# One encoder layer on one core: first norm's root moved behind the input projection, front loads cut in column blocks

## Chip, core and metric

The kernel runs on one core of one Trainium2 chip. The metric is the device time of the core in microseconds (us), lower is better. Before: 941.05 us, median of three runs (940.95 to 941.78).

## What is computed

One layer over 256 tokens of width 2048, all in fp32 (cut):

```python
xn = rmsnorm(x, norm_mix)                   # x * rsqrt(mean(x*x)+eps) * gain
p = xn @ w_in                               # 2048 x 6400, 25 units of 256 columns
yA = rwkv7_mixer(pA, ...)                   # first 7 units: token mix, LoRA, decay, state
yB = chunk_band_attention(pB)               # 6 units, 8 heads
yC = diff_attention(pC)                     # 6 units, 4 heads
yD = short_conv_mixer(pD)                   # 6 units
x = x + concat(yA, yB, yC, yD) @ w_out
x = x + hier_moe(rmsnorm(x, norm_ffn), ...) # group + top-2 of 32 experts, 192 MB of weights
return rmsnorm(x, norm_final)
```

## The kernel before

Each engine has its program, written out by hand; semaphores join them. An fp32 product is made of three float32r products: ScalarE rounds the weights (`split_hi`, L653), VectorE subtracts to get the rest (`split_lo`, L1715), TensorE forms high x high, low x high and high x low. **x** is treated likewise (`x_high` L614, `x_low` L1703).

TensorE goes through `w_in` in **granules**, a quarter of a unit's 2048 rows: 24 products of 256 columns (L1046; L1003 and L1016 in the first unit). I number them from 0: unit n is granules 4n to 4n+3, the projection 0 to 99. A granule needs `split_lo` of its number; `split_hi` of granule g needs granule g-4 used up. So both splits run three to four granules ahead at most. `advance(k)` on ScalarE and `split_lo(k)` on VectorE set by hand where splits stand between other work. Results go alternately to two PSUM banks `PJ`; unit n+2 may start when unit n is read out.

At the start VectorE and ScalarE square x (L1675, L599), GpSimd takes the root (L498), x is multiplied by it (L601, L1685, L1691) and then transposed by TensorE (L965). TensorE runs idle products until then (`warm`, L970).

Units 0 to 6 feed the RWKV mixer: `keep(n)` (ScalarE, L671) stores one share, `mix(n)` (VectorE, L1723) adds the shifted one. Between stand the LoRA products after granule 11 (L1090 to L1096, read by ScalarE L694, L697, L586), the squares' sum after granule 17 (L1103, read by ScalarE L713 after a table load), VectorE's scan (L1759), four reciprocals (L1771) and `prep_done` (L1798), for which TensorE waits after granule 32 (L1111). Units 7 to 24 are read out by ScalarE (`evac`, L586).

SyncE issues nearly all loads in one queue, in the order written. A weight load of unit n waits for granules of unit n-2. Expert units of 2 MB (one of 3 x 32 matrices) go to ten slots `wslot`; from the output projection on these are filled as memory comes free, then each as the experts release it. After the last expert the tail squares, takes two roots (GpSimd) and scales and stores both token blocks.

## Time and profile before

| | us |
|---|---|
| median of three runs | 941.05 |
| the profiled execution | 941.73 |
| its span, first to last instruction | 939.9 |
| TensorE busy | 784.9 (84%) |
| VectorE busy | 432.2 (46%) |
| ScalarE busy | 279.7 (30%) |

Times in the rows count from the start of the span. A granule or a group stands in the chain of waits when nothing later held back its end. TensorE's granted clock is 0.925 of full speed over the whole; up to 520 us each stretch shows 1.00.

### The profile page before, as it was taken

The page shows a single profiled execution, that of the slowest core. Times are in us where ns is not written, and L with a number is a line of the kernel's source. Part 1 is how long each engine was busy: PE and PEld are TensorE (multiplying, and loading weights), DVE is VectorE, ACT ScalarE, POOL GpSimd, SP SyncE. Part 2 cuts the span into 40 slices and gives each one's busy share as a digit, 9 for nine tenths or more (in the row PEclk, how much of TensorE's full clock was granted, in tenths as well). Part 3 has the DMA queues.
Part 4 walks back from the last instruction along what each step waited for, and adds up shares of the span by engine and source line. Part 5 has one row for each costly group of instructions (what it writes and reads, how often), then busy time and mean ns, then how long its engine had stood idle before and what let it go on. Part 6 is the DMA issues. An engine that isn't in the chain of part 4 may idle for free.

```text
span 939.9 us, 18496 instructions
## 1 busy us (share of the span) xinstructions
PE 784.9 (84%) x8182; PEld 633.8 (67%) x8182; DVE 432.2 (46%) x710; ACT 279.7 (30%) x457; POOL 72.3 (8%) x78
## 2 busy tenths in 40 slices
PE   8999999999999999999999775675746856468654
PEld 7999999999999999888877352343513534235332
DVE  6758947654676576845452412114131132311403
ACT  6555543433355656455410000000010000100014
POOL 3110003250000000800000000000000000000002
PEclk9999999999999999999999987798787977979778
DMA  9695544434344455799989999999999999999994
GB/s 301 208 286 153 179 133 137 128 102 135 119 148 140 136 158 178 257 344 382 383 333 412 427 427 429 426 428 425 428 426 430 424 430 425 428 427 425 428 399 178
DMA packets 84799, 285.83 MB, mean 304 GB/s; under 512 B 3834, under 2 KB 55300, under 8 KB 72300
## 3 DMA queue, kind: packets, MB, share of 16 engines
q1 hardware_dynamic: 82448, 279.20, 76.8%
q0 software_dynamic: 1568, 4.02, 1.6%
q8 instruction: 66, 1.08, 0.5%
q10 hardware_dynamic: 700, 1.39, 0.4%
q14 instruction: 17, 0.14, 0.0%
HBM read 280.37 MB, written 4.22 MB: 303 GB/s over the span
## 4 chain that ended last, share of the span: by engine, by line
PE 60%; DMA 32%; DVE 4%; ACT 2%; issue 1%; SPq 0%; POOL 0%; DVEq 0%; ACTq 0%; POOLq 0%
PE bank L1046 26%; DMA arena<-in_expert_w_up 12%; DMA arena<-in_expert_w_down 10%; DMA arena<-in_expert_w_gate 9%; PE bank L1510 8%; PE bank L1590 3%; PE bank L1063 3%; PE bank L1065 3%; PE bank L1064 3%; PE bank L965 2%; PE bank L1475 2%; PE bank L1209 1%; DVE ring_r L1715 1%; PE bank L1016 1%; PE bank L1602 1%
## 5 line engine op out<-in xcount | busy, mean ns | idle before, releaser
L1046 PE MATMUL bank<-xTr,hi 128*128 128x256 f32 x1280 | 235.7, 286 | 0.3 <-DVE ring_r L1715 0.2
L1510 PE MATMUL bank<-arena 128*32 128x256 f32 x2048 | 140.7, 442 | 106.2 <-DMA arena<-in_expert_w_up 62.9
L1046 PEld LDWEIGHTS bank<-xTr,hi 128*128 128x128 f32 x1280 | 199.3, 192 | 5.4 <-issue 3.3
L1715 DVE TENSOR_TENSOR ring_r<-arena,hi 128x1024 fp32r<-128x1024 f32 x132 | 161.8, 1236 | 87.6 <-ACT hi L653 85.1
L1510 PEld LDWEIGHTS bank<-arena 128*32 128x32 f32 x2048 | 79.2, 127 | 165.8 <-issue 137.2
L1046 PE MATMUL bank<-xTr,ring_r 128*128 128x256 f32 x640 | 181.0, 283 | 0.0
L653 ACT ACTIVATE hi<-arena 128x1024 fp32r<-128x1024 f32 x132 | 138.8, 1062 | 115.1 <-PE bank L1046 84.3
L1046 PEld LDWEIGHTS bank<-xTr,ring_r 128*128 128x128 f32 x640 | 122.7, 192 | 0.0
L2149 DVE TENSOR_TENSOR arena<-arena,bank 128x512 f32<-128x512 f32 x56 | 57.9, 1093 | 72.8 <-PE bank L1486 72.8
L894 ACT ACTIVATE g<-bank,coef 128x256 f32<-128x256 f32 x8 | 3.8, 473 | 255.1 <-PE bank L1510 255.1
L1590 PE MATMUL bank<-arena,const 128*32 128x512 f32 x448 | 54.3, 640 | 16.6 <-DMA arena<-in_expert_w_down 16.6
L2176 DVE SCALAR_TENSOR_TENSOR lora<-g,bank 128x256 f32<-128x256 f32 x8 | 3.4, 421 | 134.1 <-ACT g L894 134.1
L1475 PEld LDWEIGHTS bank<-Sel,arena 128*128 128x128 f32 x512 | 58.6, 192 | 4.4 <-issue 3.7
L1475 PE MATMUL bank<-Sel,arena 128*128 128x128 f32 x512 | 60.9, 277 | 0.4 <-issue 0.4
L2153 DVE TENSOR_TENSOR yg<-bank,yg 128x512 fp32r<-128x512 f32 x32 | 21.4, 686 | 82.6 <-ACT yg L879 82.6
L1063 PE MATMUL bank<-hi,yTr 128*128 128x512 f32 x128 | 50.4, 394 | 0.0
L1065 PE MATMUL bank<-ring_r,yTr 128*128 128x512 f32 x128 | 49.9, 390 | 0.0
L1064 PE MATMUL bank<-hi,yTr 128*128 128x512 f32 x128 | 49.8, 389 | 0.0
L1590 PEld LDWEIGHTS bank<-arena,const 128*32 128x32 f32 x448 | 17.6, 117 | 47.4 <-issue 47.4
L586 ACT ACTIVATE arena<-bank 128x512 f32<-128x512 f32 (+4 forms) x67 | 32.2, 481 | 54.4 <-PE bank L1186 23.5
L1046 PE MATMUL bank<-hi,xTr 128*128 128x256 f32 x256 | 47.8, 288 | 0.0
L879 ACT ACTIVATE yg<-bank 128x512 fp32r<-128x512 f32 x32 | 18.4, 597 | 89.5 <-PE bank L1590 71.2
(339 smaller groups left out, 885.6 us busy)
## 6 DMA issues: line engine op xcount, KB each, us to landing
arena<-in_expert_w_gate SPq DMA_DIRECT2D x30, 2048.0 KB, 29.7
arena<-in_expert_w_up SPq DMA_DIRECT2D x29, 2048.0 KB, 31.6
arena<-in_w_in SPq DMA_DIRECT2D x50, 1024.0 KB, 5.3
arena<-in_expert_w_down SPq DMA_DIRECT2D x24, 2048.0 KB, 30.3
arena<-in_w_out SPq DMA_DIRECT2D x16, 1024.0 KB, 7.8
arena<-in_expert_w_down SPq DMA_DIRECT2D x16, 512.0 KB, 8.9
arena<-in_expert_w_down SPq DMA_DIRECT2D x8, 1024.0 KB, 15.2
arena<-in_expert_w_up SPq DMA_DIRECT2D x6, 1024.0 KB, 6.3
```

Of the source, the lines that this page charges most:

```text
L586: step(A_(dst, src, ACT.Copy, **kw), signal)
L653: A_(hi[:, g % NHI, :], ring[:, n % 2, q, :], ACT.Copy).then_inc(s["hi_done"], 1)
L1046: ins = MM(PJ[n % 2][:, h * U:(h + 1) * U], a, b, start=h + q + tt + k == 0, stop=h == 1 and q == 3 and tt == 3 and k == 2)
L1063: MM(o_, yTr[:, 0, t, tok], wh[:, tt, :], start=t == 0, stop=False)
L1064: MM(o_, yTr[:, 1, t, tok], wh[:, tt, :], start=False, stop=False)
L1065: ins = MM(o_, yTr[:, 0, t, tok], wl[:, tt, :], start=False, stop=t == KT - 1)
L1475: ins = MM(bk[:, k * P:(k + 1) * P], src[:, m, t, :], Sel[:, m, :], start=m == 0, stop=m == NM - 1)
L1510: ins = MM(gu[slots_of(a), u * EH:(u + 1) * EH], xg[:, t, slots_of(a)], slot(NUQ * h + NCG * u + a)[:, t * EH:(t + 1) * EH], start=t == 0, ...
L1590: ins = MM(bank[4 + n][slots_of(a), :], hT[:, k, slots_of(a)], slot(NUQ * h + 2 * NCG + a)[:, k * DM + n * 512:k * DM + (n + 1) * 512], st ...
L1715: TT(ring_r[:, n % 2, q, :], ring[:, n % 2, q, :], hi[:, g % NHI, :].bitcast(f32), ALU.subtract).then_inc(s["lo_done"], 1)
L2149: TT(t, t, bk[:, :].rearrange("p (q t) -> p q t", t=KT), ALU.add).then_inc(s["sct_ev"], 1)
L2153: TT(buf[:, 1, :], bank[4 + n][:, :], buf[:, 0, :].bitcast(f32), ALU.subtract).then_inc(s["yg_lo"], 1)
```

## The change

- The first norm's root is no longer applied to x. x is transposed as it comes. The squares are taken later; a product of ones with a diagonal of the two roots (after granule 6) gives `R`, the root along the free axis. VectorE multiplies each mixer unit in PSUM by `R` (`scale(n)`) before `keep` and `mix` read it; the read-out of units 7 to 24 moves from ScalarE to VectorE and multiplies by the root.
- x and the first unit's weights are loaded in four pairs of 512 KB by SyncE, behind the identity matrix; TensorE takes x block by block between the first granules. The parameter loads on GpSimd wait for the last x block.
- The first expert unit is loaded one step of SyncE's loop earlier, behind a wait for the last transposed probabilities; the slots at 64 and 112 KB change places. The router's weights and gains are loaded during attention.
- Tail: the second root is taken before the first block is scaled, GpSimd and ScalarE take all four column blocks of the second token block, stored in two halves.
- In `mix`, one `split_lo` stands between `scale` and the mixing; single ones are taken out elsewhere, the one between the reciprocals among them.

```diff
@@ -363,9 +367,12 @@
 
         @block.sync
         def _(sp):
-            sp.dma_start(xs[:, 0, :], x_v[0]).then_inc(x_ld[0], 16)
-            for n, part in ((1, slice(0, DM // 2)), (2, slice(DM // 2, DM))):
-                sp.dma_start(xs[:, 1, part], x_v[1][:, part]).then_inc(x_ld[n], 16)
+            sp.dma_start(const[:, 0:P], A["const"][:, 0:P]).then_inc(const_ld, 16)
+            for q in range(4):
+                cols_ = slice(q * 512, (q + 1) * 512)
+                sp.dma_start(xs[:, :, cols_], x_cols[:, :, cols_]).then_inc(x_ld[q], 16)
+                sp.dma_start(ring[:, 0, q, :].rearrange("p (t c) -> p t c", t=4),
+                             w_in_v[:, 4 * q:4 * q + 4, order[0] * U:(order[0] + 1) * U]).then_inc(part_ld[q], 16)
...
@@ -407,10 +414,12 @@
...
-                if NU_IN + 2 <= n < NU_IN + 7:
+                if NU_IN < n < NU_IN + 6:
+                    if n == NU_IN + 1:
+                        sp.wait_ge(s["pt_ps"], NBH + NCH)
                     if n == NU_IN + 3:
                         sp.wait_ge(s["ylo_done"], YD1)
-                    moe_unit(0, n - NU_IN - 2)
+                    moe_unit(0, n - NU_IN - 1)
...
@@ -468,13 +477,11 @@
             for lo, up in ((0, 1), (1, 2), (2, 4)):
                 sp.wait_ge(s["go"], up)
                 store_out(0, lo * 512, up * 512)
-            sp.wait_ge(s["go"], 5)
-            store_out(1, 1536, 2048)
...
@@ -500,10 +507,12 @@
...
+            step(G.memset(ones_f, 1.0), s["pool_ones"])
+            pool.wait_ge(s["xt_ready"], 8)
+            for dst, src in loads:
+                pool.dma_start(dst, src).then_inc(par_ld, 16)
             rsqrt(st[:, 0:1])
             rsqrt(st[:, 1:2])
-            for dst, src in loads:
-                pool.dma_start(dst, src).then_inc(par_ld, 16)
...
@@ -545,6 +554,11 @@
...
+            pool.wait_ge(s["sm_done"], sm_count(NBH - 1))
+            pool.dma_start(gain_tp[:, :], cols(A["norm_ffn"])).then_inc(par2_ld, 16)
+            pool.dma_start(gain_pt[:, :], A["norm_ffn"].rearrange("l (p t) -> p (l t)", t=KT)).then_inc(par2_ld, 16)
+            pool.dma_start(rw[:, :, 0:NGR], A["router_group_w"].rearrange("l (t p) g -> p (l t) g", t=KT)).then_inc(par2_ld, 16)
+            pool.dma_start(rw[:, :, NGR:36], A["router_expert_w"].rearrange("l (t p) g -> p (l t) g", t=KT)).then_inc(par2_ld, 16)
             for i in range(NCH):
                 rsqrt(cst[:, :, 1:2])
...
@@ -614,32 +620,7 @@
...
-            def evac(n):
-                act.wait_ge(s["gran_used"], 4 * n + 4)
...
-                if n < NA + 12 and i < 2:
-                    copy(dst, src.rearrange("p (a m t) -> p a m t", a=2, m=2), s["pj_evac"], scale=HD ** -0.5)
-                else:
-                    copy(dst, src.rearrange("p (a b) -> p a b", a=2), s["pj_evac"])
-
-            pos = {"split": 0, "pe": 0}
...
@@ -671,11 +651,17 @@
...
-            for b in range(8):
-                if b % 2 == 0 and b < 2 * LEAD:
-                    split_hi()
-                x_high(b)
-            advance(4)
+            for q in range(4):
+                x_high(2 * q)
+                x_high(2 * q + 1)
+                split_hi()
+            split_hi()
+            square(0)
+            split_hi()
+            square(1)
+            split_hi()
+            act.wait_ge(gain_ld, 16 * NVECS + 1)
+            A_(vec[:, KT:NVEC], K[1][:, 0:NVEC - KT], ACT.Copy).then_inc(gain_ld, 1)
             keep(0)
             act.dma_start(const[:, P:], A["const"][:, P:]).then_inc(const_ld, 16)
             advance(1)
...
@@ -946,15 +932,14 @@
...
-            act.wait_ge(s["z_done"], 3)
             act.wait_ge(s["sq3_done"], 8)
-            for n in range(3):
+            for n in range(4):
+                act.wait_ge(s["z_done"], max(3, n + 1))
                 cols_ = slice(n * 512, (n + 1) * 512)
                 A_(x2n[:, 1, cols_], x2z[:, cols_], ACT.Copy, scale=st[:, 1:2]).then_inc(s["sq3_done"], 1)
-            act.wait_ge(s["sq3_done"], 10)
-            act.dma_start(out_v[1][:, 0:1024], x2n[:, 1, 0:1024]).then_inc(out_st, 16)
-            act.wait_ge(s["sq3_done"], 11)
-            act.dma_start(out_v[1][:, 1024:1536], x2n[:, 1, 1024:1536]).then_inc(out_st, 16)
+                if n % 2 == 1:
+                    act.wait_ge(s["sq3_done"], 9 + n)
+                    act.dma_start(out_v[1][:, (n - 1) * 512:(n + 1) * 512], x2n[:, 1, (n - 1) * 512:(n + 1) * 512]).then_inc(out_st, 16)
@@ -979,25 +964,23 @@
...
-            warm(26)
-            pe.wait_ge(s["scaled0"], 1)
-            for b in range(7):
-                if b == 4:
-                    pe.wait_ge(s["scaled0"], 2)
-                    pe.wait_ge(gain_ld, 16 * NVECS)
-                    nc.tensor.transpose(PJ[0][:, 0:NVEC], vec_nat, ident[0:NVEC, 0:NVEC]).then_inc(gain_ld, 1)
-                x_transpose(b, 0)
-            for b in range(7):
-                pe.wait_ge(s["scaled1"], b // 4 + 1)
-                x_transpose(b, 1).then_inc(s["xt_ready"], 1)
+            pe.wait_ge(gain3_ld, 16)
+            nc.tensor.transpose(PJ[0][:, 0:KT], gain_nat, ident[0:KT, 0:KT]).then_inc(gain3_ld, 1)
+
+            def x_block(q):
+
+                pe.wait_ge(x_ld[q], 16)
+                for b in (2 * q, 2 * q + 1):
+                    if b == 7:
+                        pe.wait_ge(s["xlo_done"], 2)
+                    x_transpose(b, 0)
+                    x_transpose(b, 1).then_inc(s["xt_ready"], 1)
 
...
@@ -1017,12 +1000,15 @@
...
+            x_block(0)
+            x_block(1)
             for q in range(4):
                 first_high(q)
                 first_low(q)
-                if q == 0:
-                    x_transpose(7, 0)
-                    x_transpose(7, 1).then_inc(s["xt_ready"], 1)
+                if q < 2:
+                    x_block(q + 2)
+            pe.wait_ge(gain_ld, 16 * NVECS)
+            nc.tensor.transpose(K[1][:, 0:NVEC - KT], vec_nat, ident[0:NVEC - KT, 0:NVEC - KT]).then_inc(gain_ld, 1)
...
@@ -1077,7 +1063,13 @@
...
-            granules(4)
+            granules(3)
+            pe.wait_ge(s["diag_done"], NM)
+            pe.wait_ge(s["pool_ones"], 3)
+            for m in range(NM):
+                ins = MM(K[2][:, m * P:(m + 1) * P], ones_f, diag[:, m, :], start=True, stop=True)
+            ins.then_inc(s["ones_ps"], 1)
+            granules(1)
...
@@ -1670,31 +1662,6 @@
...
-            half = slice(DM // 2, DM)
-            step(TS(xs[:, 0, half], xs[:, 0, half], st[:, 0:1], None, ALU.mult), s["scaled0"])
-            v.wait_ge(s["sq1_done"], 2)
-            step(TT(st[:, 1:2], st[:, 1:2], st[:, 2:3], ALU.add))
-            variance(1)
-            v.wait_ge(s["rstd_done"], 2)
-            for half in (slice(0, DM // 2), slice(DM // 2, DM)):
-                step(TS(xs[:, 1, half], xs[:, 1, half], st[:, 1:2], None, ALU.mult), s["scaled1"])
-            v.wait_ge(gain_ld, 16 * NVECS + 2)
...
@@ -1704,6 +1671,29 @@
...
+            def evac(n):
+                v.wait_ge(s["gran_used"], 4 * n + 4)
...
+                if n < NA + 12 and i < 2:
+                    step(STT(dst, PJ[n % 2][:, :].rearrange("p (a m t) -> p a m t", a=2, m=2), HD ** -0.5,
+                             R[:, :].rearrange("p (m t) -> p m t", m=2).unsqueeze(1).to_broadcast([P, 2, 2, P]), ALU.mult,
+                             ALU.mult), s["pj_evac"])
+                    return
+                by = st[:, 0:NM].unsqueeze(2) if order[n] in natural else R[:, :].unsqueeze(1)
+                step(TT(dst, PJ[n % 2][:, :].rearrange("p (a b) -> p a b", a=2), by.to_broadcast([P, 2, U]), ALU.mult),
+                     s["pj_evac"])
...
@@ -1714,22 +1704,54 @@
...
+                    if q == 3 and NA <= n - 1 < NU_IN - 1:
+                        evac(n - 1)
...
+            def scale(n):
+
+                v.wait_ge(s["gran_used"], 4 * n + 4)
+                t = PJ[n % 2][:, :].rearrange("p (h t) -> p h t", h=2)
+                step(TT(t, t, R[:, :].unsqueeze(1).to_broadcast([P, 2, SEQ]), ALU.mult), s["pj_scaled"])
 
             def mix(n):
 
+                scale(n)
+                split_lo(1)
                 for h in range(2):
                     i = 2 * order[n] + h
                     v.wait_ge(s["mix1"], 2 * n + 2)
                     step(STT(mA[:, i, 1:], PJ[n % 2][:, h * SEQ:(h + 1) * SEQ - 1], mu[:, i:i + 1], mA[:, i, 1:],
                              ALU.mult, ALU.add), s["mixA"])
 
-            for b in range(8):
-                x_low(b)
-                if b % 2 == 1 and b < 2 * LEAD:
-                    split_lo(1)
-            split_lo(4)
+            for q in range(4):
+                x_low(2 * q)
+                x_low(2 * q + 1)
+                split_lo(1)
+            split_lo(1)
+            square(0)
+            split_lo(1)
+            square(1)
+            split_lo(1)
+            v.wait_ge(s["sq1_done"], 2)
+            step(TT(st[:, 0:NM], st[:, 0:NM], st[:, NM:2 * NM], ALU.add))
+            for m in range(NM):
+                variance(m)
+            for m in range(NM):
+                v.wait_ge(s["rstd_done"], m + 1)
+                step(TS(diag[:, m, :], ident, st[:, m:m + 1], None, ALU.mult), s["diag_done"])
+            v.wait_ge(gain_ld, 16 * NVECS + 2)
+            step(TS(omu[:, :], mu, -1.0, 1.0, ALU.mult, ALU.add), s["prep"])
+            step(TS(w0h, w0h, 0.5, None, ALU.mult), s["prep"])
+            step(TS(a0h, a0h, 0.5, None, ALU.mult), s["prep"])
+            step(TS(ok_a[:, :], k_a, -1.0, 1.0, ALU.mult, ALU.add), s["prep"])
+            v.wait_ge(s["ones_ps"], 1)
+            step(V.tensor_copy(R[:, :], K[2][:, 0:SEQ]))
             mix(0)
-            split_lo(1)
...
@@ -1745,12 +1767,12 @@
             mix(1)
             for c in range(2):
                 step(TS(kk[:, c, :], k_[:, c, :], k_k[:, c:c + 1], None, ALU.mult))
-            split_lo(4)
+            split_lo(3)
             mix(2)
             for c in range(2, 4):
                 step(TS(kk[:, c, :], k_[:, c, :], k_k[:, c:c + 1], None, ALU.mult))
             step(TT(kmod, kk, kk, ALU.mult), s["kr_done"])
-            split_lo(2)
+            split_lo(1)
             flat = [t.rearrange("p a b -> p (a b)") for t in (decay, chunk_start, Pc)]
             step(V.memset(chunk_start, 1.0))
             step(TS(iclr, iclr, 0.5, 0.5, ALU.mult, ALU.add))
             split_lo(1)
             mix(3)
-            split_lo(1)
             split_lo(2)
             v.wait_ge(s["knorm_done"], 2)
...
             mix(4)
             for c in range(AT):
                 step(V.reciprocal(kmod[:, c, :], kmod[:, c, :]))
-                if c == 1:
-                    split_lo(1)
             split_lo(1)
             step(TT(kk, kk, kmod, ALU.mult), s["kr_done"])
             split_lo(1)
...
             mix(5)
-            split_lo(1)
             step(V.memset(flat[1][:, 0::CH], 1.0))
             split_lo(1)
...
             step(TT(iclr, iclr, kk, ALU.mult))
-            split_lo(1)
             step(TT(bh, iclr, Pinv, ALU.mult))
...
@@ -2223,16 +2240,12 @@
             add_last(3)
             v.wait_ge(s["sq3_done"], 7)
             variance3(0)
-            v.wait_ge(gain3_ld, 16)
-            v.wait_ge(s["rstd_done"], NRSTD - 1)
-            scale_psum(0)
             v.wait_ge(s["sq3_done"], 8)
             variance3(1)
-            for n in range(1, 4):
+            v.wait_ge(gain3_ld, 34)
+            v.wait_ge(s["rstd_done"], NRSTD - 1)
+            for n in range(4):
                 scale_psum(n)
-            v.wait_ge(s["rstd_done"], NRSTD)
-            cols_ = slice(3 * 512, 4 * 512)
-            STT(x2n[:, 1, cols_], x2n[:, 1, cols_], st[:, 1:2], gain3[:, cols_], ALU.mult, ALU.mult).then_inc(s["go"], 1)
             assert step.count[s["var_ready"]] == NRSTD
```

**ScalarE, after the first unit** (L653 and L637 are `split_hi`; L671 and L651 `keep`; L613 the squares). Before:

```order
L614 ACTIVATE xTr<-bank,vec 128x256 x8
L653 ACTIVATE hi<-arena 128x1024 x4
L671 ACTIVATE arena<-bank,omu 128x256 x2
L680 DMA const<-in_const 128x992
L653 ACTIVATE hi<-arena 128x1024
L683 ACTIVATE arena<-arena 64x256
```

and now:

```order
L637 ACTIVATE hi<-arena 128x1024 x2
L613 ACTIVATE arena,st<-arena 128x1024
L637 ACTIVATE hi<-arena 128x1024
L613 ACTIVATE arena,st<-arena 128x1024
L637 ACTIVATE hi<-arena 128x1024
L664 ACTIVATE vec<-bank 128x46
L651 ACTIVATE arena<-bank,omu 128x256 x2
L666 DMA const<-in_const 128x992
L637 ACTIVATE hi<-arena 128x1024
L669 ACTIVATE arena<-arena 64x256
```

Seven splits stand before `keep(0)` both times; `keep(0)` now waits for `scale(0)`, and that for the product with ones.

**VectorE, from the fourth to the fifth mixer unit** (L1715 and L1705 are `split_lo`, L1723 and L1728 `mix`, L1719 `scale`). Before:

```order
L1767 TENSOR_SCALAR arena<-arena 128x1024
L1715 TENSOR_TENSOR ring_r<-arena,hi 128x1024
L1723 SCALAR_TENSOR_TENSOR arena<-bank,vec,arena 128x255 x2
L1771 RECIPROCAL arena<-arena 128x256 x2
L1715 TENSOR_TENSOR ring_r<-arena,hi 128x1024
L1771 RECIPROCAL arena<-arena 128x256 x2
L1715 TENSOR_TENSOR ring_r<-arena,hi 128x1024
L1775 TENSOR_TENSOR arena<-arena 128x1024
```

and now:

```order
L1788 TENSOR_SCALAR arena<-arena 128x1024
L1705 TENSOR_TENSOR ring_r<-arena,hi 128x1024
L1719 TENSOR_TENSOR bank<-bank,Sel 128x512
L1705 TENSOR_TENSOR ring_r<-arena,hi 128x1024
L1728 SCALAR_TENSOR_TENSOR arena<-bank,vec,arena 128x255 x2
L1792 RECIPROCAL arena<-arena 128x256 x4
L1705 TENSOR_TENSOR ring_r<-arena,hi 128x1024
L1794 TENSOR_TENSOR arena<-arena 128x1024
```

The split of granule 23 has moved ahead of the mixing and all four reciprocals now stand before that of granule 24.

**VectorE, from the third mixer unit to the scan** (L1752 and L1774 the squares of k, L1759 and L1781 the scan). Before:

```order
L1723 SCALAR_TENSOR_TENSOR arena<-bank,vec,arena 128x255 x2
L1751 TENSOR_SCALAR arena<-arena,vec 128x256 x2
L1752 TENSOR_TENSOR arena<-arena 128x1024
L1715 TENSOR_TENSOR ring_r<-arena,hi 128x1024 x2
L1755 MEMSET arena 128x1024
```

and now:

```order
L1719 TENSOR_TENSOR bank<-bank,Sel 128x512
L1705 TENSOR_TENSOR ring_r<-arena,hi 128x1024
L1728 SCALAR_TENSOR_TENSOR arena<-bank,vec,arena 128x255 x2
L1773 TENSOR_SCALAR arena<-arena,vec 128x256 x2
L1774 TENSOR_TENSOR arena<-arena 128x1024
L1705 TENSOR_TENSOR ring_r<-arena,hi 128x1024
L1777 MEMSET arena 128x1024
```

The mixing and the squares now stand behind the split of granule 15.

## Rows read from the trace of the kernel before

**Rows 1.** The page, chain that ended last, shares by engine.
```profile
PE 60%; DMA 32%; DVE 4%; ACT 2%; issue 1%; SPq 0%; POOL 0%; DVEq 0%; ACTq 0%; POOLq 0%
```

**Rows 2.** Chain of waits, 0 to 130 us: start, length, what.
```profile
0.73 5.38 DMA arena<-in_x
...
15.07 1.19 PE bank L1003 x8
...
27.66 11.52 PE bank L1046 x96
...
60.80 1.07 ACT hi L653
...
69.91 3.14 PE bank L1046 x24
73.05 1.74 PE bank L1103 x8
...
98.30 20.42 PE bank L1046 x168
118.72 1.68 PE bank L1111 x16
```

**Rows 3.** The same chain, in the experts.
```profile
523.82 21.50 DMA arena<-in_expert_w_up
...
869.22 32.90 DMA arena<-in_expert_w_up
```

**Rows 4.** Timeline, 0 to 15 us: start, length, engine, line, operation.
```profile
1.41 6.96 PE L970 MATMUL bank<-ones 128*128 128x128 bf16 x78 [1.41 <-POOL ones L502]
...
13.40 1.57 ACT L614 ACTIVATE xTr<-bank,vec 128x256 fp32r<-128x256 f32 x4
```

**Rows 5.** VectorE's groups, 27 to 120 us: busy us, mean ns.
```profile
L1715 DVE TENSOR_TENSOR ring_r<-arena,hi 128x1024 fp32r<-128x1024 f32 x31 | 37.7, 1224 | 17.1 <-ACT hi L653 16.4
L1771 DVE RECIPROCAL arena<-arena 128x256 f32<-128x256 f32 x4 | 7.0, 1751 | 0.1
L1723 DVE SCALAR_TENSOR_TENSOR arena<-bank,vec,arena 128x255 f32<-128x255 f32 x14 | 6.7, 480 | 3.0 <-ACT arena L671 2.7
L1759 DVE TENSOR_TENSOR_SCAN arena<-arena 128x1024 f32<-128x1024 f32 x1 | 2.3, 2291 | 0.0
...
L1755 DVE MEMSET arena<- 128x1024 f32 x1 | 0.9, 912 | 0.2 <-issue 0.2
...
L1751 DVE TENSOR_SCALAR arena<-arena,vec 128x256 f32<-128x256 f32 x2 | 0.7, 353 | 0.1
L1758 DVE TENSOR_SCALAR arena<-arena 128x1024 f32<-128x1024 f32 x1 | 0.7, 694 | 0.0
```

**Rows 6.** Timeline of ScalarE, 39 to 78 us.
```profile
39.21 0.84 ACT L671 ACTIVATE arena<-bank,omu 128x256 f32<-128x256 f32 x2 [1.75 <-PE bank L1046]
...
74.86 1.28 ACT L713 ACT_TABLE_LOAD   x1 [1.03 <-PE bank L1103]
76.16 1.23 ACT L713 ACTIVATE arena<-bank 128x512 f32<-128x512 f32 x2
```

**Rows 7.** VectorE on 128x512 with one side in PSUM: timeline at 147 us.
```profile
147.88 0.68 DVE L1822 TENSOR_TENSOR arena<-bank,const 128x512 f32<-128x512 f32 x1
```

**Rows 8.** The page, costliest groups: the same form in the experts.
```profile
L2149 DVE TENSOR_TENSOR arena<-arena,bank 128x512 f32<-128x512 f32 x56 | 57.9, 1093 | 72.8 <-PE bank L1486 72.8
```

**Rows 9.** Windows: from:to, us, busy of each engine, PEclk, DMA share, GB/s.
```profile
250.00:300.00 50.00, 50.00 (x460) 47.19 (x459) 35.75 (x77) 27.92 (x51) 1.64 (x1) 1.00 0.45 144
380.00:385.00 5.00, 5.00 (x34) 4.55 (x33) 2.65 (x5) 2.72 (x4) 4.64 (x5) 1.00 0.48 157
485.00:490.00 5.00, 4.64 (x46) 4.06 (x48) 4.26 (x22) 0.37 (x2) 0.00 (x0) 1.00 1.00 364
490.00:495.00 5.00, 5.00 (x76) 3.32 (x65) 2.93 (x12) 0.00 (x0) 0.00 (x0) 1.00 0.80 273
```

**Rows 10.** Timeline of the tail: GpSimd's root, ScalarE's and VectorE's scaling, last store.
```profile
932.05 0.55 POOL L498 TENSOR_TENSOR st<-st,mhalf 128x1 f32<-128x1 f32 x1 [1.28 <-DVE st L2207]
932.64 1.95 ACT L953 ACTIVATE arena<-arena,st 128x512 f32<-128x512 f32 x3 [2.12 <-POOL st L498]
933.92 0.74 DVE L2235 SCALAR_TENSOR_TENSOR arena<-arena,st 128x512 f32<-128x512 f32 x1
...
934.61 0.38 ACTq L957 DMA_DIRECT2D out<-arena  x1
```

More of the change, by code:

```diff
@@ L243, in build @@
         t5_dram = nc.dram_tensor("t5_scratch", [4, SPAN], f32)
-        x_ld = [sem(f"x_ld{m}") for m in range(NM + 1)]
+        x_ld = [sem(f"x_ld{m}") for m in range(3)]
         gain_ld, par_ld, par2_ld, par3_ld, const_ld = (sem(n) for n in ("gain_ld", "par_ld", "par2_ld", "par3_ld", "const_ld"))
@@ L252, in build @@
         x2_st = [sem(f"x2_st{n}") for n in range(4)]
-        tail_ld = [sem(f"tail_ld{n}") for n in range(3)]
+        part_ld = [sem(f"part_ld{n}") for n in range(3)]
         gain3_ld, x2o_ld, out_st = sem("gain3_ld"), sem("x2o_ld"), sem("out_st")
+        x_ld.append(x2o_ld)
+        part_ld.append(out_st)
         rel_st, bias_ld = sem("rel_st"), sem("bias_ld")
@@ L383, in store_x2 @@
                 sp.dma_start(x2_cols[:, :, nb * 512:(nb + 1) * 512], x2b[nb % 3]).then_inc(x2_st[nb], 16)
-            for n in range(NU_IN + NU_OUT):
+            for n in range(1, NU_IN + NU_OUT):
                 for half in range(2):
@@ L818, in _ @@
             advance(1)
-            advance(NG_IN - pos["pe"] + 3)
+            advance(NG_IN - (pos["split"] - LEAD) + 3)
             act.wait_ge(s["dconv0"], 1)
@@ L845, in _ @@
             for nb in range(3):
-                advance(NG_IN + 8 * (nb + 1) - pos["pe"])
+                advance(NG_IN + 8 * (nb + 1) - (pos["split"] - LEAD))
                 square_block(nb)
@@ L851, in _ @@
                 rows_permuted(nb)
-            advance(NG - pos["pe"])
+            advance(NG - (pos["split"] - LEAD))
             act.wait_ge(s["wo_ev"], 7)
@@ L1452, in _ @@
             MM(bank[5][:, 0:NE], ones[:, :], em[:, 0, :], start=True, stop=False)
-            MM(bank[5][:, 0:NE], ones[:, :], em[:, 1, :], start=False, stop=True).then_inc(s["total_ps"], 1)
+            MM(bank[5][:, 0:NE], ones[:, :], em[:, 1, :], start=False, stop=True).then_inc(s["ones_ps"], 1)
             def sel_transpose(q):
@@ L1839, in _ @@
                 if i in (1, 2):
-                    step(V.memset(S[i - 1], 0.0), s["halves_zero"])
+                    step(V.memset(S[i - 1], 0.0), s["diag_done"])
                 if i == 3:
```

124 lines of the change are left out of this document (49 added, 75 removed).

## The prediction

> **What bounds the kernel now.** I read the shares of the chain first, then the chain in order of time, then the groups and the timeline of VectorE and ScalarE between 27 and 120 us, the windows around the start of the experts, and the tail. TensorE holds 60% of the chain and DMA 32% [rows 1]: up to about 520 us TensorE sets the pace, after that the stream of expert weights [rows 3], which runs without a break until its last wait ends at 902.1 (869.22 + 32.90). The stream cannot start before TensorE has gone through both projections and the router, since the ten slots are full by then. So whatever moves TensorE's path before 500 us moves the end by as much, and the change has to be judged by that path.
>
> On it, the first product stands at 15.07, the first unit ends at 27.66, and a granule takes 2.88 us (11.52 for 96 products, four granules) [rows 2]. Four marks show how little room VectorE has in the mixer: the split behind ScalarE's at 60.80 leads to granule 17 at 69.91; the squares' sum ends at 74.79 (73.05 + 1.74); granule 26 starts at 98.30 behind VectorE; granule 33's predecessor ends and the bonus sums start at 118.72 [rows 2]. TensorE's need of granule 24 is 74.79 + 6 x 2.88 = 92.1. VectorE's busy share of 46% over the whole says nothing here.
>
> **The change, part by part.** A minus is earlier.
>
> 1. *The start.* Removed are squares, two roots and the scaling of x ahead of the transposes. Now TensorE makes 52 idle products instead of 78, to 1.41 + 52 x 0.089 = 6.05 [rows 4]; the first x block, 0.57 MB with the identity, should have landed by then, as the first 1 MB took 5.38 [rows 2]. Then transposes and the gain 0.5, four scaled copies 1.57 [rows 4], a split 1.07 [rows 2], handovers 0.3: first product at 9.5. From first product to the end of the unit it was 12.6 (15.07 to 27.66); twelve more transposes stand between, at most 0.12 each as a product of twice their width, so 14.0 at most, and 13.0 if the gaps of before close. I take 13.7, end 23.2: -4.5 (bounds -5.2 and -4.0).
>
> 2. *Granule 7.* This is where the new dependency bites. ScalarE's split of granule 7 stands behind `keep(0)`, that behind `scale(0)`, that behind the copy of `R`, that behind the product with ones after granule 6. After granule 6 TensorE waits for: ones 0.4, copy of R 0.4 (priced as one 256-wide PSUM read, half of 0.84 in rows 6), scale 0.69, keep 0.84 [rows 6], split on ScalarE 1.07, split on VectorE 1.22 [rows 5], five handovers of 0.05 or so and the issue of a load: 5.0. The scale writes PSUM, which no row shows; the nearest are 0.68 [rows 7] and, for the same width among the experts, 1.09 [rows 8]. I take 0.69, for rows 7 is from the stage of the mixer; with 1.09 seven scales cost 2.8 more, which is in the range. +5.0. Granule 8 follows behind mix 0.96, two activations 0.84, both splits 2.3 and gaps 0.3, 4.4 together, against 2.88 and the small T5 product 0.7 on TensorE: +0.8. The first three terms leave +1.3: the start is given back.
>
> 3. *Granule 17.* Before, mix, the two products with k_k and the squares of the third unit stood ahead of ScalarE's LoRA work, in free time. Now mix stands behind the split of granule 15, which ScalarE makes at 60.80 only [rows 2]. From there: splits 15 and 16, memset 0.91, 0.69, scan 2.29, split 17 gave 69.7, what the chain shows. Inserted are 0.96 + 0.71 + 1.22 = 2.9 [rows 5]. Covered by nothing: +2.8.
>
> 4. *Granules 24 to 26*, counted as if 1 to 3 had not been. Splits 17 and 18 end at 71.5. scale(3) 0.69, keep(3) 0.84; then ScalarE has three exponentials with splits 19 and 20 between (each 1.07 as a 1024-wide split) and a small one: 78.6. Table load 1.28 and roots 1.23 [rows 6]: 81.1, where before they began at 74.86 with the sum. Split 21 on both engines 83.4, maximum 0.69, split 22 85.3, scale(4) 86.0, keep 86.8, split 23 89.1, mix 90.1, four reciprocals at 1.75 and gaps [rows 5] 97.4, split 24 98.6. TensorE wants it at 92.1. Granule 26 follows at 104.4 against 98.30: +6.1. The split that stood between the reciprocals was what held 92.1; with scale(4) tied to the end of granule 19, even without the lateness the split 24 would come 1.8 too late.
>
> 5. *To the bonus sums.* VectorE from split 26 on: seven splits 8.5, two scales 1.4, twice the wait for keep and ScalarE's split 3.8, mixes 1.9, four 256-wide operations 2.0, five of 1.22, small ones 0.5: 24.2. So 128.5 against 118.72, of which 6.1 is counted: +3.6.
>
> 6. *The rest of the projection.* Eighteen read-outs at 0.69 go to VectorE. TensorE is not late anywhere here before, VectorE is busy 72% in the attention [rows 9]. Hidden mostly by three granules of lead, 8.6 us; if that cover is gone a read-out can cost its 0.69, all of them 12. I take +1.0 (0 to 4).
>
> 7. *The first expert unit* is issued some 10 us earlier, when the queues are half idle (share 0.48 [rows 9]), and it no longer crowds the output projection; the wait for the probabilities is over by the time SyncE reaches it, so nothing behind it in SyncE's queue is late. But it frees no slot: at 490 to 495 the DMA share drops to 0.80, the slots being full and waiting for the experts. An emptier queue earlier makes that gap longer. 0. The router's loads in attention: four issues on GpSimd ahead of the third kind of root, hidden; 0.
>
> 8. *The tail.* The second root ended at 932.60 [rows 10], now right behind the first at 931.6. ScalarE's three scalings move 1.0 earlier, a fourth (0.65) and an issue of 0.38 come in; VectorE loses 0.74. The last issue, 934.6 before [rows 10], stays within 0.2, but more is on its way by then: -0.6 (0 to -1.5).
>
> Sum: -4.5 + 5.8 + 2.8 + 6.1 + 3.6 + 1.0 - 0.6 = +14.2. The profiled execution took 941.73, its span and 1.8 around it; 955.9. It lies 0.7 above the median of the runs, so against them I say **955.2**.
>
> **The rivals.** (a) *The early expert unit pays after all*, the stream starting with less outstanding. For it: the share is 1.00 at 485 to 490. Against: the gap behind it. 2.1 MB at the 364 GB/s of that window are 5.8 us: 949.4. (b) *Attention runs dry too*: read-outs delay the softmax on VectorE and TensorE waits at each head, 4 us more: 959. For it: 72%. Against: TensorE's products fill its path there without a pause. (c) *The front's small loads are slow*: x block 3 lands late. If each of the four pairs took the 5.38 of the first 1 MB, the last is there at 22.2, and the unit ends behind transposes, copies, two splits and 24 products, 7.2 later, at 29.4: 6 us more, 961. Against it: the rate before did not wait for one transfer to end before the next. The Trainium skill, DMA: Bandwidth & Descriptors, section Bandwidth, asks for batches of 1 MiB or more, for three quarters of the peak; by that rule the 512 KB blocks speak against this change, and no row here shows one alone. (d) *The other side*: the leads hold. VectorE stood idle 17.1 us ahead of its splits between 27 and 120 [rows 5]. If that idle time takes up the scales, keeps and moved mixes, and the `R` product is ready so that granule 7's split is in time, only the start and tail count: 941.05 - 5.1 = 935.9. It decides at granule 24: if its split is there within 92.1 less the gain. Against: the idle time lies where VectorE waits for ScalarE, which now waits for VectorE. (e) *Gains and losses cancel* (the change does in effect nothing): the waits return only what the start gives, 941.
>
> **How the numbers follow.** Forecast 0.66, (a) 0.09, (b) 0.08, (c) 0.03, (d) 0.10, (e) 0.04. Around the forecast, the bounds of the terms (start, PSUM price, read-outs, tail) and a margin of a few tenths per chained step give 950 to 960. Taking in (a) and (b) and leaving out (c), (d) and (e): **946 to 961**. About 0.2%, 1.9 us, is what a measurement can tell from no change: faster 0.10, same 0.04, slower 0.86 (forecast, a, b, c).
>
> **What would show it.** First product at 9 to 10, first unit done by 24. A stall of TensorE of about 5 us before granule 7 in the chain, with ScalarE's `keep` and both splits; one of near 3 before granule 17; VectorE's four reciprocals in the chain and a stall of 6 before granule 24; `prep_done` ahead of the bonus sums at 132. The start of the output projection and every expert wait some 15 later than before, at equal spacing. Wrong would be: no reciprocals in the chain, or the last expert wait ending before 905.

## The result, and the profile after

The changed kernel takes 960.34 us (median of four runs, 959.54 to 961.26) against 941.24 in the same session, a ratio of 1.0197 (1.0184 to 1.021). The prediction said 955.2, range 946 to 961; its own bounds for the forecast, 950 to 960, were just passed. The profiled execution took 960.65, its span is 958.7, 18.8 longer than before. TensorE's granted clock is 0.923 over the whole (0.925 before).

The chain of waits of the changed kernel up to the attention, its longest pieces (start us, us, what; L1032 is the granule's product, L1719 `scale`, L637 and L1705 the splits, L699 ScalarE's table load, L1792 the reciprocals, L1103 the bonus sums, L950 transposes behind them). It answers to [rows 2]:

```profile
23.42 8.83 PE bank L1032 x72
...
33.26 0.71 DVE bank L1719
34.72 1.06 ACT hi L637
35.88 1.24 DVE ring_r L1705
37.16 5.33 PE bank L1032 x24
...
43.22 11.71 PE bank L1032 x96
...
84.88 1.28 ACT L699
...
96.31 1.76 DVE arena L1792
98.10 1.76 DVE arena L1792
99.88 1.76 DVE arena L1792
101.67 1.76 DVE arena L1792
...
109.65 1.23 DVE ring_r L1705
110.88 0.62 DVE bank L1719
...
134.81 1.95 PE bank L1103 x16
136.76 4.17 PE bank L950 x24
140.92 8.79 PE bank L1032 x72
```

Between 58.8 and 134.8 us no piece is TensorE's; before, it had those from 69.91 to 74.80 and from 98.30 to 118.72. Two pieces have the wrong length for their work. Granule 7 takes 5.33 us for 24 products where a granule takes 2.88, and the 24 transposes behind the bonus sums take 4.17 where they took 2.68. The windows say why (columns: stretch, length, busy us and count of TensorE, its weight load, VectorE, ScalarE, GpSimd, granted clock, DMA share, GB/s):

```profile
32.00:37.00 5.00, 0.69 (x7) 0.50 (x5) 2.25 (x3) 1.78 (x3) 0.00 (x0) 0.83 0.77 257
37.00:43.00 6.00, 5.84 (x26) 5.21 (x26) 4.76 (x14) 3.78 (x5) 0.42 (x1) 0.57 0.01 2
...
97.00:110.00 13.00, 8.20 (x49) 7.99 (x48) 11.48 (x9) 3.46 (x5) 0.00 (x0) 0.75 0.40 132
...
138.00:140.00 2.00, 2.00 (x11) 2.00 (x10) 0.30 (x1) 1.97 (x3) 0.00 (x0) 0.50 0.00 0
```

TensorE stood still from 32.7 to 37.16. At 36 to 37 us its granted clock was 0.50, which is 1.2 GHz, and it came back to 1.00 (2.4 GHz) between 42 and 43:

```profile
36.00:37.00 1.00, 0.00 (x0) 0.00 (x0) 1.00 (x1) 0.00 (x0) 0.00 (x0) 0.50 0.73 298
...
42.00:43.00 1.00, 1.00 (x6) 0.37 (x4) 0.97 (x2) 0.00 (x0) 0.42 (x1) 0.91 0.00 0
```

Before, each stretch up to 520 us showed 1.00. The clock fell to 0.50 in two more places, around 77 and from 104 to 110 us (in the window 97 to 110), each time with TensorE's wait for a split. The chain ran through ScalarE and VectorE there, so no piece of it is longer for these two.

Where ScalarE and VectorE stand in each other's way (timeline; in brackets the idle time before, and its releaser; L651 is `keep`):

```profile
78.76 0.84 ACT L651 ACTIVATE arena<-bank,omu 128x256 f32<-128x256 f32 x2 [8.87 <-DVE bank L1719]
```

```profile
113.41 1.23 DVE L1705 TENSOR_TENSOR ring_r<-arena,hi 128x1024 fp32r<-128x1024 f32 x1 [1.92 <-ACT hi L637]
```

`keep(3)` waited 8.87 us for `scale(3)`, which VectorE has behind the scan and two splits. In units 5 and 6 VectorE waits 1.92 us between scale and mixing, as the split it has there comes on ScalarE behind `keep`.

And the end, from the last expert wait on (chain), answering to [rows 3] and [rows 10]:

```profile
890.68 31.60 DMA arena<-in_expert_w_up
...
934.96 10.60 DMA arena<-in_norm_final
...
945.74 1.29 POOL arena L587
...
950.62 0.56 POOL st L505
...
951.20 1.34 ACT arena L939 x2
```

Set against the rows of before, the 18.8 us come from these places. "Adds" is what a mark lost more than the mark above it:

| place | mark before, after | adds | predicted |
|---|---|---|---|
| first unit's end | 27.66, 23.42 | -4.2 | -4.5 |
| to the LoRA products: ones 0.5, wait 4.5, granule 7 at half clock 2.4 | 51.54, 54.86 | +7.6 (0.2 between products) | +5.8 |
| split of granule 17 starts | 68.63, 75.03 | +3.1 | +2.8 |
| split of granule 26 starts | 97.02, 109.65 | +6.2 | +6.1 |
| bonus sums | 118.72, 134.81 | +3.5 | +3.6 |
| behind them: half clock 1.7, the sums 0.3 longer (1.95 for 1.68) | 134.09, 152.08 | +1.9 | 0 |
| attention up to 280 us | 260.80, 280.39 | +1.6 | } +1.0 |
| last softmax of the differential attention | 279.15, 299.30 | +0.6 | } |
| router to last expert wait's end | 902.12, 922.28 | 0 | 0 |
| tail | 939.9, 958.7 | -1.4 | -0.6 |

### The profile page after: what moved, and what is told of

Read it like the earlier page. It is cut to its first block, busy times and chain, and to the rows that moved or that the text cites. A ratio compares the mean times of both kernels' runs of the same rounds, so it can differ in the third digit from the quotient of the medians.

```text
span 958.7 us, 18481 instructions
## 1 busy us (share of the span) xinstructions
PE 788.3 (82%) x8161; PEld 639.0 (67%) x8161; DVE 447.5 (47%) x733; ACT 270.2 (28%) x440; POOL 73.2 (8%) x80
## 4 chain that ended last, share of the span: by engine, by line
PE 55%; DMA 33%; DVE 6%; ACT 3%; issue 2%; SPq 1%; POOL 1%; ACTq 0%; DVEq 0%; POOLq 0%
PE bank L1032 23%; DMA arena<-in_expert_w_up 12%; DMA arena<-in_expert_w_gate 9%; DMA arena<-in_expert_w_down 9%; PE bank L1502 8%; PE bank L1582 3%; PE bank L1049 3%; PE bank L1051 3%; PE bank L1050 3%; PE bank L950 2%; PE bank L1467 2%; DVE ring_r L1705 1%; DMA arena<-in_norm_final 1%; PE bank L1201 1%; PE bank L999 1%
## 5 line engine op out<-in xcount | busy, mean ns | idle before, releaser
L1032 PE MATMUL bank<-xTr,hi 128*128 128x256 f32 x1280 | 242.1, 291 | 12.2 <-DVE ring_r L1705 12.2
L1032 PEld LDWEIGHTS bank<-xTr,hi 128*128 128x128 f32 x1280 | 204.6, 197 | 17.5 <-DVE ring_r L1705 13.0
L1705 DVE TENSOR_TENSOR ring_r<-arena,hi 128x1024 fp32r<-128x1024 f32 x132 | 163.2, 1244 | 94.9 <-ACT hi L637 92.4
L1032 PE MATMUL bank<-xTr,ring_r 128*128 128x256 f32 x640 | 183.6, 287 | 0.0
L637 ACT ACTIVATE hi<-arena 128x1024 fp32r<-128x1024 f32 x132 | 138.1, 1059 | 104.4 <-PE bank L1032 78.9
L1032 PEld LDWEIGHTS bank<-xTr,ring_r 128*128 128x128 f32 x640 | 125.7, 196 | 0.0
L2166 DVE TENSOR_TENSOR arena<-arena,bank 128x512 f32<-128x512 f32 x56 | 57.9, 1096 | 74.1 <-PE bank L1478 74.1
L1032 PE MATMUL bank<-hi,xTr 128*128 128x256 f32 x256 | 47.6, 287 | 0.6 <-DVE ring_r L1705 0.6
L1032 PEld LDWEIGHTS bank<-hi,xTr 128*128 128x128 f32 x256 | 39.7, 191 | 2.1 <-DVE ring_r L1705 1.2
```

Of the source, the lines that this page charges most:

```text
L637: A_(hi[:, g % NHI, :], ring[:, n % 2, q, :], ACT.Copy).then_inc(s["hi_done"], 1)
L1032: ins = MM(PJ[n % 2][:, h * U:(h + 1) * U], a, b, start=h + q + tt + k == 0, stop=h == 1 and q == 3 and tt == 3 and k == 2)
L1705: TT(ring_r[:, n % 2, q, :], ring[:, n % 2, q, :], hi[:, g % NHI, :].bitcast(f32), ALU.subtract).then_inc(s["lo_done"], 1)
L2166: TT(t, t, bk[:, :].rearrange("p (q t) -> p q t", t=KT), ALU.add).then_inc(s["sct_ev"], 1)
```

## The experiments

All times are medians against the kernel before in the same session (941.24, 941.65 and 941.28 us).

**1. The tail alone.** The tail's hunks of the diff on the kernel before.

> The kernel before with only the tail's new order. From the last expert wait to the end of the span it was 37.8 us before (902.1 to 939.9) and 36.4 after the whole change (922.3 to 958.7): if the tail's order makes that, 1.4 us less than before, about 939.8. The prediction's term says 0.6 less, 940.6. If the shorter end comes from elsewhere (the state of the queues or of the clock there), no difference, 941.2.

Measured: 940.45, ratio 0.9986 (0.9976 to 0.9995). The gain is real and about 0.8 to 1.3 us; the prediction's 0.6 lies in the interval, the 1.4 of the trace as well. In its profiled execution the first product behind the last expert wait starts at 901.88 and the span ends at 939.2, so 37.3 us remain, where it was 37.6 before (from 902.25) and 36.3 after (from 922.42): one trace doesn't show so small a gain, and the 1.4 above may be partly chance.

**2. The expert slot and the router's loads alone.**

```diff
-                if NU_IN + 2 <= n < NU_IN + 7:
+                if NU_IN < n < NU_IN + 6:
+                    if n == NU_IN + 1:
+                        sp.wait_ge(s["pt_ps"], NBH + NCH)
```

> The kernel before with only the first expert unit one step earlier, the two slots exchanged and the router's loads in attention. The prediction's term: no difference, 941.2 within 0.5, the last expert wait ending at 902 as before. Rival (a), the unit pays because the stream starts with 2 MB less outstanding: 5.8 us less, 935.4, with the last expert wait ending at 896. Third: the loads in attention delay a weight load of the projection: 0.3 to 1 slower, and a new DMA wait in the chain between 200 and 480 us.

Measured: 941.24, ratio 0.9999 (0.999 to 1.0008). Term 7 holds and rival (a) falls: the 2 MB earlier bought nothing. That this is so because the stream later waits for memory to come free is the prediction's argument, and no run tests it.

**3. TensorE kept busy in two waits of the changed kernel.**

```diff
             ins.then_inc(s["ones_ps"], 1)
+            for _ in range(44):
+                MM(K[4][:, 0:P], ones[:, :], ones[:, :], start=True, stop=True)
             granules(1)
```

and 12 of them ahead of the wait for `prep_done`.

> The changed kernel with 44 idle products of 128 columns in TensorE's wait before granule 7 and 12 before the bonus sums; nothing waits for them and they end within the waits. Theory: the granted clock fell to 0.50 behind each wait (37 to 42 us, 138 to 141 us) and cost 2.4 us and 1.8 us there, on the path: the clock stays at 1.00, granule 7 takes 2.9 instead of 5.3 us, the end comes 4.3 earlier, 956.0. Rival: the low clock has another cause (what the other engines do in those stretches), it stays at 0.50 and the time stays at 960.3. Half-way: one of the two waits only, 957.9 or 958.5.

Measured: 958.28, ratio 1.0181 (1.0168 to 1.0195), 2.1 us less by the medians, half of what the theory said; by the intervals anything from nothing to 3 us less is possible. Windows of this run, behind the first wait and behind the bonus sums:

```profile
37.00:43.00 6.00, 5.84 (x31) 4.95 (x32) 4.75 (x14) 3.79 (x5) 0.40 (x1) 0.72 0.03 7
...
135.00:140.00 5.00, 5.00 (x47) 5.00 (x47) 3.21 (x5) 3.33 (x5) 0.00 (x0) 1.00 0.01 3
```

and its chain:

```profile
37.16 4.57 PE bank L1032 x24
...
134.09 1.95 PE bank L1107 x16
136.04 2.68 PE bank L950 x24
138.71 8.62 PE bank L1032 x72
```

Behind the bonus sums the clock stayed at 1.00 and the transposes took 2.68 again, 1.7 us less together with the products behind them. That the 12 idle products did it isn't shown. Without them TensorE waited 1.24 us there in experiment 5 and 1.66 in experiment 12, against 1.42 in the changed kernel, and in both the clock stayed at 1.00 as well. What made it fall in this one place is open.

At granule 7 the idle products ended at 35.2, and the clock fell all the same (1.00 in the window 37 to 38, 0.50 from 39 on). The granule took 4.57 instead of 5.33, but this too need not be the idle products' doing: with the same wait of 4.46 us and nothing in it the granule took 4.45 in experiment 4 and 5.49 in experiment 12. So 44 small products in the wait did not hold the clock; experiment 5 takes the wait away. This trace has none of the gaps in the attention described under experiment 12 either, which is a good part of its 3.5 us shorter span.

**4. The splits where they stood before.** In the changed kernel: no split between `scale` and mixing but in unit 0, one between the reciprocals again.

```diff
                 step(V.reciprocal(kmod[:, c, :], kmod[:, c, :]))
+                if c == 1:
+                    split_lo(1)
             split_lo(1)
```

> The changed kernel with VectorE's splits where they stood before, the scales staying: none between scale and mixing but in unit 0, one between the reciprocals again, mix(2) ahead of split 15. Theory: the moved splits cost the 3.05 us at granule 17 and most of what was lost at granule 24; split 26 ends at 106.3 instead of 110.9, and the two waits of 1.9 us between scale and mixing of units 5 and 6 shrink by 1 us each: 6.6 less, 953.7. Rival: the order matters little, since keep, the exponentials and mixing wait for the scale whatever the order: less than 2 us, 958.5 or more.

Measured: 952.13, ratio 1.0126 (1.0109 to 1.0143): 8.2 us less than the whole change by the medians, 6.7 by the two ratios. The theory's 6.6 can't be told from either; the rival is out. Chain:

```profile
37.85 4.45 PE bank L1032 x24
...
94.56 1.22 DVE ring_r L1705
...
105.47 1.23 DVE ring_r L1705
...
128.74 1.95 PE bank L1103 x16
130.69 2.68 PE bank L950 x24
```

From the LoRA products to the bonus sums it took 74.1 us instead of 79.9 (54.66 to 128.74): that 5.9 is the part of the order. Granule 7 was 0.9 shorter with the same stall, the start 0.7 later, and the transposes behind the sums run at full clock, which the order of the splits need not have caused (see experiment 3). So the place of the splits was 6 to 8 of the 19 us, and these need no root to be lost.

**5. Granule 7 given its lead.**

```diff
-            granules(3)
+            granules(2)
             pe.wait_ge(s["diag_done"], NM)
...
-            keep(0)
             act.dma_start(const[:, P:], A["const"][:, P:]).then_inc(const_ld, 16)
             advance(1)
+            keep(0)
```

and VectorE's split of granule 7 ahead of the copy of `R`.

> The changed kernel with the product of ones behind granule 5 (the diagonals are there at 28.9 us) and both splits of granule 7 ahead of keep(0) and of the copy of R. Theory: the stall of 4.9 us and the half clock behind it go, and granule 8 is not late: the LoRA products start at 47.6 instead of 54.9, and since all that follows hangs on them, the end comes 7.3 earlier, 953.0. Rival: another wait takes its place before granule 7 or 8 (the weight load, or mixing of unit 0): half of it or less, 956.7 or more.

Measured: 954.73, ratio 1.0145 (1.0129 to 1.016), 5.6 less, between the theory and its rival. TensorE's waits up to 50 us are down to this one, before granule 8:

```profile
37.87 0.50 PE L1032 MATMUL bank<-xTr,hi 128*128 128x256 f32 x2 [0.95 <-DVE ring_r L1705]
```

Stall and half clock are gone (1.00 in every window from 30 to 50 us), the LoRA products start at 49.58, 5.3 earlier. This shows that the stall was the cause of the long granule. The missing 2 us are, for the most part, a start that was 0.6 later in this run (the transposed vectors at 23.79 instead of 23.16) and granule 8, whose split on ScalarE stood behind the tanh.

**6. The start alone, root left out of the mixer.** Order of experiment 4, and no `scale`; units 0 to 6 are computed without the root.

> The changed kernel without the seven scales (the mixer's units go without the root, so the output is another one) and with VectorE's splits where they stood before; R is still made for the read-outs. It shows what the start is worth if the root cost nothing. Theory: the 4.3 us of the start reach the end: 941.2 - 4.3 + 0.6 for the read-outs - 0.8 for the tail = 936.7, the clock at 1.00 up to 500 us. Rival: something behind the start does not follow (weight loads, the exponentials, the reciprocals), 939 to 941.

Measured: 939.29, ratio 0.9975 (0.9964 to 0.9985), the rival. Of the 4.3 us of the start, 3.0 are left at the LoRA products (48.58) and 2.1 at the bonus sums (116.42, by the start of their first product; 118.56 before). On the way to the LoRA products go the ones (0.46) and this, for ScalarE issues the rest of the constants behind `keep(0)`, and that waits for `omu`, now ready at 29.3:

```profile
36.15 0.80 PE L1076 MATMUL bank<-arena,t5t 32*4 32x384 f32 x2 [0.50 <-DMA const<-in_const]
```

So even with no scaling of the mixer's units the whole kernel is 2.4 us faster, not 4.3, and of these about 1 is the tail's (experiment 1).

**7. All the work of the change, woven in another order.** Product of ones and splits as in 5, split 8 ahead of the tanh, and:

```diff
@@ ScalarE
-            keep(3)
             step(A_(lam[:, 2:4], lam[:, 0:2], ACT.Exp), s["lam_exp"])
...
             step(A_(flat[2], flat[2], ACT.Exp), s["scan_ready"])
+            keep(3)
@@ VectorE
+            scale(4)
             for c in range(AT):
                 step(V.reciprocal(kmod[:, c, :], kmod[:, c, :]))
+                if c == 0:
+                    mix(4)
+                if c == 1:
+                    split_lo(1)
...
             step(TT(kk, kk, kmod, ALU.mult), s["kr_done"])
             split_lo(1)
+            scale(5)
             v.wait_ge(s["scan_ready"], 3 + AT)
```

> The changed kernel with all its work, in another order: product of ones behind granule 5, splits 7 and 8 ahead, keep(3) behind the exponentials, and each scale put where VectorE waited or had other work to do before mixing (scale(4) ahead of the first reciprocal, scale(5) in the wait for the four identities). Theory: of the seven scales only scale(4) lies on the path: 941.2 - 4.3 + 0.5 (ones) + 0.65 + 0.6 (read-outs) - 0.8 (tail) = 937.9. Rival: the root's work on VectorE cannot be hidden in any order, since it was busy without a pause from 97 to 118 before: 4 scales on the path and waits for keep, 941 or more.

Measured: 939.61, ratio 0.9978 (0.9969 to 0.9987): faster than before, by 2.0 us, and 20.7 less than the change with the same work. The theory's 937.9 was missed, and the rival's 941 as well. It computes the full layer and is as fast as experiment 6, which has no scaling in the mixer but stands in the old order, with the ones behind granule 6; what the scalings cost in the order of 7 no run prices. About 1 of the 2.0 is the tail's. The granted clock was 1.00 up to 500 us. Chain:

```profile
94.32 1.24 DVE ring_r L1706
95.60 20.41 PE bank L1033 x168
116.01 1.68 PE bank L1104 x16
117.69 2.68 PE bank L951 x24
```

TensorE has its piece of 168 products again, and the bonus sums stand at 116.01, 2.7 earlier than before. Of these, 1.3 go up to the last softmax of the differential attention, 1.0 of it in two gaps of the kind described under experiment 12, and 0.6 in it.

**8. The scan's fills moved ahead of `scale(1)`,** otherwise as 7.

> As the run before it, with the two fills of the scan's start vector (0.91 and 0.07 us) moved from behind split 16 to ahead of scale(1), where VectorE waits. Theory: they stood on the path from the LoRA work to granule 17 and beyond: 0.9 less, 937.0. Rival: TensorE, not VectorE, sets the end there once the front is out of the way: no difference.

Measured: 939.3, ratio 0.9972 (0.996 to 0.9985), no difference from 7 that can be told; the theory's 937.0 is out. From the LoRA products to the bonus sums it took 66.9 instead of 67.8, so the fills did stand on the path there. But the LoRA products stand 1.0 later, 0.45 of it from a later start (23.31 against 22.86) and the rest from a new wait before granule 11:

```profile
46.01 0.50 PE L1033 MATMUL bank<-xTr,hi 128*128 128x256 f32 x2 [0.51 <-DVE ring_r L1706]
```

There was no idle time where the fills were put: in 7 VectorE goes from a split straight on to `scale(1)` at 39.66. Here `scale(1)` starts at 41.24, and the split of granule 11, queued behind it, is late. The fills gave 0.8 in one place and took 0.5 in another.

**9. The ones behind granule 6 again,** otherwise as 7.

> The order of e7_weave (939.6), with the product of ones behind granule 6 again; splits 7 and 8 stay ahead. In e7_weave TensorE waited for the diagonals behind granule 5 (first T5 product at 35.58, where 35.1 was the sum). Theory: that wait goes, the LoRA products start 0.6 earlier, 939.0. Rival: R and with it keep and mixing of unit 0 come 2.9 us later and granule 8 waits for them: 0.5 or more slower, 940.1.

Measured: 942.5, ratio 1.0012 (1.0003 to 1.0021), 2.9 worse than 7: the rival, and more than it said.

```profile
38.66 0.51 PE L1033 MATMUL bank<-xTr,hi 128*128 128x256 f32 x2 [1.68 <-DVE ring_r L1706]
```

VectorE waited 1.9 us for the ones, until 33.4, and split 8 stood behind `scale` and mixing of unit 0. This one choice, the product of ones one granule earlier, takes the kernel from 1.2 us slower than before to 2.0 faster.

**10. Read-outs one split later,** otherwise as 7.

> The order of e7_weave (939.6), with each read-out of units 7 to 24 on VectorE one split later. Theory: of the read-outs only one lies on the path, that in the last softmax of the differential attention (0.69 at 265.6 us), and it moves behind the split for which TensorE waits there: 939.0. Rival: read-outs come late for the next unit but one and TensorE waits for them: slower by 0.3 to 0.7 each, 941 or more.

Measured: 939.28, ratio 0.9977 (0.9967 to 0.9986). No difference from 7 that can be told, though 939.0 lies in the interval as well; the rival is out. In the last softmax TensorE now waits 0.61 for the read-out itself instead of 0.65 for the split behind it: the 0.6 moved, and stayed.

**11. Experiments 9 and 10 together, with the fills of 8 in yet another place,** behind the mixing of unit 1, ahead of splits 11 to 14.

> e9_ones6 and e10_late together, with the two fills of the scan's start vector moved ahead of splits 11 to 14, where VectorE waits: the best version so far by theory, 0.6 + 0.6 + 0.4 (half of the 0.9 of the fills, TensorE taking over the path) less than 939.6: 938.0, below both kernels. Rival: TensorE's own work and its unexplained gaps set the end by now, 939.0 or more.

Measured: 941.56, ratio 1.0002 (0.9993 to 1.0012). The expected 938.0 was missed by 3.6. The wait before granule 8 is that of 9 (1.68), and one of 0.49 before granule 11 is there as in 8. From the LoRA products on it took 66.6 instead of 67.8 to the bonus sums. What read-outs and fills each add can't be told apart here. The best order stays that of 7, with or without the fills of 8.

**12. The read-outs on ScalarE again.** The changed kernel; units 7 to 24 are read out without the root.

> The changed kernel with the read-outs of units 7 to 24 back on ScalarE and without the root (units 7 to 24 go unscaled), each behind the split where VectorE has it. It prices the read-outs. Theory: only the one in the last softmax counts, 0.6: 959.7, and the three gaps of 0.5 us on TensorE between 187 and 211 us, for which the profile shows no releaser, have another cause. Rival: the gaps come from the read-outs: 2.1 less, 958.2.

Measured: 959.33, ratio 1.019 (1.0177 to 1.0204), 0.6 to 1.0 less than the change, near the theory; but the rival's 958.2 lies in the interval too, and in its trace the clock stays at 1.00 behind the bonus sums (1.5 us less) while the front is 0.8 later. So the time doesn't decide, the trace does. The wait of 0.64 in the last softmax is gone, and the stretch that ends there takes 18.35 us as before the change, where it took 18.91. A gap is still there (waits of TensorE, 155 to 262 us), and the changed kernel had these:

```profile
PE bank L1224 <- issue: 0.5, 1, 0.5
```

```profile
PE bank L1201 <- issue: 0.8, 2, 0.5
PE bank L1192 <- issue: 0.2, 1, 0.2
```

They lie in the midst of series of 64x64 products in the mixer's state updates, with no releaser. The kernel before, and experiments 1 to 3, show none in that stretch; 4 to 12 show 0.2 to 1.6 us. Experiment 3 has all the read-outs on VectorE and no gap, this one has none there and a gap. So they are not the read-outs' doing. What they are stays open.

## Why the prediction was right, and where not

The sign, the place and the mechanism were right, and the time lies in the range, 5 us above the forecast. That it does so is in part luck: the forecast's own bounds ended at 960, and the range went to 961 to take in the rivals (a) and (b), of which (a) did not come and (b), waits in the attention of 4 us, only with 0.6. What filled the room was a cost that no term had.

- *Start.* -4.5, measured -4.2. The first x block landed by 6.0 as assumed (issued at 1.19, 4.8 us), and its transposes began at 6.09. The sum had the first product behind that block alone, but the program transposes two blocks ahead of it, and the second landed at 8.86: first product at 9.75, not 9.5. Rival (c), slow small loads, did not come: behind the first product no x block held up the first unit. Its rule, that of the Trainium skill, DMA: Bandwidth & Descriptors, section Bandwidth, is neither confirmed nor refuted: the first 512 KB took 4.8 us, where 1 MB took 5.38 [rows 2], both with other loads queued behind them, and in the first 12 us 3.28 MB were moved in all, 3.41 before. That the smaller blocks brought the first product forward isn't shown: the first of x lands no earlier than before (6.0 against 6.11), and what went are the squares, the root and the scaling ahead of the transposes.
- *Granule 7.* The wait was 4.46 and the ones 0.46, 4.9 together against 5.0. The scale took 0.70 in PSUM (0.69 taken). The 0.8 for granule 8 did not come, but only as the long granule hid it: the split of granule 8 ended at 41.33 us, and at full clock TensorE would have wanted it at 40.77 (37.16 + 2.88 + 0.73). So what the half clock added to the path there is, by this estimate, 1.9 us (granule 8 began at 43.22 and not at 41.37) and not 2.4. **The step that failed stands here**: no term had the clock. "A granule takes 2.88" was carried over a stall of 5 us, and the granule behind it took 5.33. No row of before up to 520 us had a stall of that length on TensorE. But the same trace has such stalls in the experts: TensorE waited 9.1 us up to 545.46, its granted clock was 0.50 from 540 to 549, and the 0.925 over the whole comes from there. The prediction could have read it off and priced it. The Trainium skill, TensorE: Matmul & The Clock Gate, section Why this matters for your kernels, warns of idle gaps between bursts of products, behind which the clock is back at half rate. The trace of after agrees (0.50 in the windows from 36 to 42 us); the prediction forecast such a gap and did not draw that conclusion.
- *Granule 17* +3.1 against +2.8, *granules 24 to 26* +6.2 against +6.1, *to the bonus sums* +3.5 against +3.6. Experiment 4 shows that the order of the splits was most of it. ScalarE's `keep(3)` waited 8.87 us for `scale(3)` with three exponentials queued behind it.
- *Behind the bonus sums* the clock cost 1.7 again, not predicted, and 0.3 more went with the sums. With the 1.9 at granule 7 the clock makes 3.6 of the 4.6 us that the span went beyond +14.2.
- *Read-outs.* +1.0 (0 to 4): measured 0.6, at one place. The 1.6 of gaps (1.0 of idle time, the rest in the products beside it) were in no term; the tail's -1.4 offset most of them by chance.
- *Expert slot and router loads.* 0, measured 0.0 with an interval of 0.9 us to each side.
- *Tail.* -0.6 (0 to -1.5), measured alone -0.8 to -1.3.
- *Rival (d)*, that the leads hold, was wrong for the order of this change, and right for the work: experiment 7 has the same added work in VectorE's idle time and is faster than before. The text against it, that this idle time lies where the two engines wait for each other, was an argument on the order, not on the work.

## What to carry to other kernels

When work is moved to an engine with idle time, ask per instruction what it waits for and what is queued behind it: seven scalings of 0.70 us and the splits moved with them cost 19 us in one order, and in another the same work left the kernel 2.0 us faster than before. Put a split or any other work that others wait for ahead of a wait where it can go there, and put the new operation where the engine waited already, but then look at what is queued next (the fills of experiment 8 made a later split late). Count a stall of TensorE of some microseconds as longer than it is, for the products behind it may run at half clock.

## What was not expected of the hardware

- TensorE's granted clock went from 1.00 to 0.50 in a stand-still of 4.5 us and was back 3 to 6 us after its end (40.8 to 43.5 us). The same stall had another price in each trace: the 24 products behind it took 5.33, 4.45 (experiment 4) and 5.49 us (experiment 12) instead of 2.88. With 2.6 us of small products at the head of that wait the clock fell too, and they took 4.57.
- Behind the bonus sums, after a wait of 1.4 us and 16 products of two columns, it fell in the changed kernel, but not behind 1.24 us (experiment 5) or 1.66 us (experiment 12) in the same place. So the length of the wait alone does not tell.
- A product series of 64x64 can pause for 0.2 to 1.4 us with no releaser in the profile, in one order of the program and not in another.
- VectorE's `scale`, which reads 128x512 from PSUM and writes it back there, took 0.70 us, as an operation of that width that only reads PSUM did (0.68 [rows 7]).
